# Attention by head pairs and transposes by row halves in a hybrid decoder step on one NeuronCore

## What is computed

```python
for layer in range(DEPTH):                                   # DEPTH = 2
    xp = layer_norm(ALPHA * xp + 0.5 * swiglu(xp, *f1), ...)  # xp prompt, xs samples, same weights
    if layer % 2 == 0:
        qa, ka, va, qb, kb, vb, gb = ab_project(xp, pos_p, w_in_ab[li])
        attn = moba_prompt(qa, ka, va, pos_p)      # per head: softmax(q k^T / 8 + causal mask) v
        attn_s = moba_sample(qa_s, ka_s, va_s, cache_k[li], cache_v[li], page_table, pos_s)
        ...                                        # retention, output projection
    else:
        mix_p, a_re, a_im = s5_layer(xp, ...)      # u: 64 groups x 16 channels, scan over time
    xp = layer_norm(ALPHA * xp + mix_p, ...)
    xp = layer_norm(ALPHA * xp + 0.5 * swiglu(xp, *f2), ...)
```

## Time and profile before

| what | value |
|---|---|
| time, median of 3 runs | 2546.82 us |
| lowest and highest | 2542.66 and 2546.82 us |
| the profiled execution's own time | 2551.39 us |
| its span, first to last instruction | 2549.4 us |
| TensorE busy, share of the span | 2436.4 us, 96% |
| VectorE, ScalarE, GpSimd | 64%, 43%, 18% |
| mean granted TensorE clock | 0.984 |
| DMA, mean | 164 GB/s |

### The profile page before, as it was taken

The page is one execution under the profiler, slowest core; times in us unless marked ns, Lnnn a source line. Parts: engine busy times, 40 slices in busy tenths (PEclk is TensorE's granted clock), DMA queues, the critical chain, the costliest instruction groups (busy, mean ns, idle before and its releaser), DMA issues.

```text
span 2549.4 us, 45472 instructions
## 1 busy us (share of the span) xinstructions
PE 2436.4 (96%) x18347; PEld 2287.9 (90%) x18347; DVE 1631.8 (64%) x2584; ACT 1085.4 (43%) x1645; POOL 457.9 (18%) x532
## 2 busy tenths in 40 slices
PE   7998999999999999999999999999999989999998
PEld 7988998998788767789999999999999889999997
DVE  5887776657665545577686657467656575486555
ACT  3433455333454333353253534455433537354333
POOL 4886700002100021300110201021001000121000
PEclk9999999999999999999899999999999999999999
DMA  8667776444354787644456556555555556555553
GB/s 178 177 176 191 196 198 191 132 122 118 113 152 122 231 256 238 176 124 135 118 169 188 155 150 190 184 160 151 149 152 144 168 173 211 154 154 148 153 150 98
DMA packets 676274, 417.26 MB, mean 164 GB/s; under 512 B 31554, under 2 KB 639682, under 8 KB 676066
## 3 DMA queue, kind: packets, MB, share of 16 engines
q1 hardware_dynamic: 669538, 393.98, 53.8%
q0 software_dynamic: 6528, 20.37, 2.6%
HBM read 395.51 MB, written 18.78 MB: 163 GB/s over the span
## 4 chain that ended last, share of the span: by engine, by line
PE 77%; DVE 12%; issue 3%; ACT 3%; SPq 2%; DMA 2%; POOL 0%; POOLq 0%; ACTq 0%; DVEq 0%
PE ps L256 20%; PE ps L258 19%; PE ps L257 19%; DVE w_lo L251 4%; PE ps L881 2%; PE ps L882 2%; PE ps L883 2%; ACT w_hi L242 2%; PE ps L2259 1%; PE ps L1582 1%; PE ps L1624 1%; PE ps L1597 1%; DMA w_raw<-in_ffn_w_up 1%; PE ps L1069 1%; SPq L1938 1%
## 5 line engine op out<-in xcount | busy, mean ns | idle before, releaser
L251 DVE TENSOR_TENSOR w_lo<-w_raw,w_hi 128x1024 fp32r<-128x1024 f32 (+1 forms) x648 | 823.2, 1275 | 631.3 <-ACT w_hi L242 628.5
L256 PE MATMUL ps<-x_hi,w_hi 128*128 128x256 f32 (+1 forms) x3200 | 968.0, 302 | 37.3 <-DVE w_lo L251 30.7
L257 PE MATMUL ps<-x_lo,w_hi 128*128 128x256 f32 (+1 forms) x3200 | 954.4, 298 | 0.0
L258 PE MATMUL ps<-x_hi,w_lo 128*128 128x256 f32 (+1 forms) x3200 | 954.3, 298 | 0.0
L242 ACT ACTIVATE w_hi<-w_raw 128x1024 fp32r<-128x1024 f32 (+1 forms) x648 | 669.2, 1034 | 540.0 <-PE ps L258 380.2
L256 PEld LDWEIGHTS ps<-x_hi,w_hi 128*128 128x128 f32 x3200 | 615.1, 192 | 54.5 <-DVE w_lo L251 40.7
L257 PEld LDWEIGHTS ps<-x_lo,w_hi 128*128 128x128 f32 x3200 | 615.4, 192 | 1.1 <-issue 0.2
L258 PEld LDWEIGHTS ps<-x_hi,w_lo 128*128 128x128 f32 x3200 | 614.7, 192 | 0.0
L256 PE MATMUL ps<-h_hi,w_hi 128*128 128x256 f32 (+1 forms) x1408 | 424.7, 302 | 13.8 <-DVE w_lo L251 10.9
L257 PE MATMUL ps<-h_lo,w_hi 128*128 128x256 f32 (+1 forms) x1408 | 414.8, 295 | 0.0
L258 PE MATMUL ps<-h_hi,w_lo 128*128 128x256 f32 (+1 forms) x1408 | 414.7, 295 | 0.0
(11 more groups left out here) (263 smaller groups left out, 2265.3 us busy)
## 6 DMA issues: line engine op xcount, KB each, us to landing
w_raw<-in_ffn_w_gate SPq DMA_DIRECT2D x176, 512.0 KB, 4.2
w_raw<-in_ffn_w_up SPq DMA_DIRECT2D x176, 512.0 KB, 3.9
w_raw<-in_ffn_w_down SPq DMA_DIRECT2D x128, 512.0 KB, 3.7
w_raw<-in_w_in_ab SPq DMA_DIRECT2D x56, 512.0 KB, 3.9
w_raw<-in_ffn_w_down SPq DMA_DIRECT2D x64, 384.0 KB, 3.3
arena<-in_cache_k SPq DMA_DIRECT2D x64, 256.0 KB, 3.7
arena<-in_cache_v POOLq DMA_DIRECT2D x64, 256.0 KB, 4.4
w_raw<-in_w_out_ab SPq DMA_DIRECT2D x16, 512.0 KB, 3.7
```

The source lines that it names most:

```text
L251: dve.tensor_tensor(T.w_lo[:, u % RING, 0:n], T.w_raw[:, u % RAW, 0:n], T.w_hi[:, u % RING, 0:n].bitcast(F32), ALU.subtract).then_inc(T.w_ ...
L256: pe.matmul(out, w_hi, m_hi, start=first, stop=False)
L257: pe.matmul(out, w_hi, m_lo, start=False, stop=False)
L258: return pe.matmul(out, w_lo, m_hi, start=False, stop=last)
```

## The change

Four things change; line numbers of the new kernel are given as L1056 and so on in the listings below.
- **Prompt attention by pairs.** A job is two heads (p) of one tile: 8 jobs and 11 steps for each of `att_a` and `att_b`. The two heads' scores stand one behind the other, on the two row halves, into banks `LOW` and `HIGH`. Every 128x128 turn of probabilities becomes two turns of 64 rows into `TURN` and `NORM_BANK`. Probabilities are held once, not twice; mask, maximum and shift are one VectorE instruction for both heads; the exponential and the move are two ScalarE instructions for a pair. A tile's output is turned into `LOW`, and the next scores, which need that bank, stand in the same step behind it.
- **Key pages by row halves.** A step turns its two pages together: 16 turns of 64 rows, alternating between the lower half (into `NORM_BANK`, moved by ScalarE) and the upper half (into `TURN`, moved by VectorE). It waits for both pages and for both moves of the step before. A slot is free when the step that turned it has ended.
- **S5 inputs by row halves.** 16 turns of 64 rows in place of 8, lower half into bank 4, upper into bank 5, and two ScalarE copies of half the size.
- **Samples' steps singly.** `slowly` in place of `paired`: of each 8 steps from step 8 on, the first four (softmax, turn of the probabilities, first values) stand behind an FFN step of their own, the other steps in twos. That makes 31 FFN steps in place of 22. As `att_b` takes 11 steps in place of 19, the samples now stand behind the 12th to the 42nd step of `f1a`; the first five of these are down steps.

```diff
--- before.py
+++ after.py
...
-        self.jobs = [(i, h) for i in tiles for h in range(HEADS)]
+        self.jobs = [(i, p) for i in tiles for p in range(PAIRS)]
         n = self.N = len(self.jobs)
...
-        k, r = divmod(s - lag - 2 - (HEADS - 1), HEADS)
+        k, r = divmod(s - lag - 2 - (PAIRS - 1), PAIRS)
...
-                if h == 0 and k:
+                if p == 0 and k:
...
+                for e in range(2):
+                    h = 2 * p + e
+                    for j in range(i + 1):
...
-                for j in range(self.jobs[n][0] + 1):
-                    mm = pe.transpose(T.ps[:, TURN, j * P:(j + 1) * P], self.prob[:, n % 2, j * P:(j + 1) * P],
-                                      T.ident[:, :])
+
+                for e in range(2):
+                    for j in range(self.jobs[n][0] + 1):
+                        for half in range(2):
+                            at = (4 * e + j) * HD
+                            mm = pe.transpose(T.ps[:, self.turns[half], at:at + HD],
+                                              self.prob[HALF[half], e, j * P:(j + 1) * P], T.ident[HALF[half], HALF[half]])
             k = self.last(s, 1)
             if k is not None:
                 pe.wait_ge(T.pa_normed.h, self.normed + k + 1)
                 pe.wait_ge(T.pa_expd.h, self.expd + min(s, self.N))
...
             if s < self.N:
-                i, h = self.jobs[s]
-                if s >= 2:
-                    pe.wait_ge(T.pa_expd.h, self.expd + s - 1)
-                k = self.last(s - 1, 1)
+                i, p = self.jobs[s]
+                if s:
+                    pe.wait_ge(T.pa_expd.h, self.expd + s)
                 if k is not None and self.put is None:
                     pe.wait_ge(T.pa_rested.h, self.rested + k + 1)
                 elif k is not None:
                     pe.wait_ge(T.pa_rounded.h, self.rounded + k + 1)
-                rows = HALF[h % 2]
-                pe.matmul(T.ps[:, LOW + s % 2, 0:(i + 1) * P], M.qaT[self.g][rows, h // 2, local(self.g, i)],
-                          M.kaT[rows, h // 2, 0:(i + 1) * P], start=True, stop=True).then_inc(T.pa_scored.h, 1)
+                for e in range(2):
+                    mm = pe.matmul(T.ps[:, LOW + e, 0:(i + 1) * P], M.qaT[self.g][HALF[e], p, local(self.g, i)],
+                                   M.kaT[HALF[e], p, 0:(i + 1) * P], start=True, stop=True)
+                mm.then_inc(T.pa_scored.h, 1)
...
+            if s < self.N:
+                i = self.jobs[s][0]
+                two = slice(2 * s, 2 * s + 2)
+                dve.wait_ge(T.pa_scored.h, self.scored + s + 1)
+                diag = T.ps[:, LOW:LOW + 2, i * P:(i + 1) * P]
+                T.dve_chain(dve, dve.tensor_tensor(diag, diag, M.causal[:, :].unsqueeze(1).to_broadcast([P, 2, P]), ALU.add))
+                T.dve_chain(dve, dve.tensor_reduce(self.top[:, two], T.ps[:, LOW:LOW + 2, 0:(i + 1) * P], AX_X, ALU.max))
+                dve.tensor_scalar(self.shift[:, two], self.top[:, two], -HD ** -0.5, None, ALU.mult)\
+                   .then_inc(T.pa_maxed.h, 1)
...
+                tiles = slice(0, self.jobs[n][0] + 1)
                 act.wait_ge(T.pa_turned.h, self.turned + n + 1)
-                if n >= 2:
-                    act.wait_ge(T.pa_valued.h, self.valued + n - 1)
-                act.activation(self.prob_t[:, n % 2, 0:w], T.ps[:, TURN, 0:w], ACT.Copy).then_inc(T.pa_moved.h, 1)
+                if n:
+                    act.wait_ge(T.pa_valued.h, self.valued + n)
+                for half in range(2):
+                    last = act.activation(
+                        self.prob_t.rearrange("p e (j h t) -> p h e j t", h=2, t=HD)[:, half, :, tiles],
+                        T.ps[:, self.turns[half], :].rearrange("p (e j t) -> p e j t", e=2, t=HD)[:, :, tiles], ACT.Copy)
+                last.then_inc(T.pa_moved.h, 1)
...
                 act.wait_ge(T.pa_maxed.h, self.maxed + s + 1)
-                if s >= 2:
-                    act.wait_ge(T.pa_turned.h, self.turned + s - 1)
-                act.activation(self.prob[:, s % 2, 0:w], T.ps[:, LOW + s % 2, 0:w], ACT.Exp,
-                               bias=self.shift[:, s:s + 1], scale=HD ** -0.5, accum_out=self.total[:, s:s + 1])\
-                   .then_inc(T.pa_expd.h, 1)
+                if s:
+                    act.wait_ge(T.pa_turned.h, self.turned + s)
+                for e in range(2):
+                    at = slice(2 * s + e, 2 * s + e + 1)
+                    last = act.activation(self.prob[:, e, 0:w], T.ps[:, LOW + e, 0:w], ACT.Exp, bias=self.shift[:, at],
+                                          scale=HD ** -0.5, accum_out=self.total[:, at])
+                last.then_inc(T.pa_expd.h, 1)
...
             if i >= slots:
-                q.wait_ge(T.sa_k_turned.h, i - slots + 1)
+                q.wait_ge(T.sa_k_turned.h, (i - slots) // 2 + 1)
             q.dma_start(self.k_slots[i % slots], src).then_inc(self.k_slot_loaded[i % slots].h, 16)
...
-    def turn_keys(self, pe, i):
+    def turn_keys(self, pe, s):
+
         T = self.T
         slots = len(self.k_slots)
-        pe.wait_ge(self.k_slot_loaded[i % slots].h, (i // slots + 1) * 16)
-        if i >= 2:
-            pe.wait_ge(T.sa_k_moved[i % 2].h, i // 2)
+        for i in (2 * s, 2 * s + 1):
+            pe.wait_ge(self.k_slot_loaded[i % slots].h, (i // slots + 1) * 16)
+        if s:
+            for moved in T.sa_k_moved:
+                pe.wait_ge(moved.h, s)
         for p in range(PAIRS):
-            mm = pe.transpose(T.ps[:, (NORM_BANK, TURN)[i % 2], p * P:(p + 1) * P],
-                              self.k_slots[i % slots][:, p * P:(p + 1) * P], T.ident[:, :])
+            for i in range(2):
+                for half in range(2):
+                    at = (i * PAIRS + p) * HD
+                    mm = pe.transpose(T.ps[:, (NORM_BANK, TURN)[half], at:at + HD],
+                                      self.k_slots[(2 * s + i) % slots][HALF[half], p * P:(p + 1) * P],
+                                      T.ident[HALF[half], HALF[half]])
...
-            for i in (2 * s, 2 * s + 1):
-                if i < BP * 2 * PAGES:
-                    self.turn_keys(pe, i)
-            yield
-
-    def move_keys(self, eng, copy, i):
+            if s < BP * PAGES:
+                self.turn_keys(pe, s)
+            yield
...
+    def move_keys(self, eng, copy, s, half):
+
         T = self.T
-        b, r = divmod(i, PAGES)
+        b, r = divmod(2 * s, PAGES)
         b2, j = divmod(r, GP)
         if b:
             eng.wait_ge(T.sa_scored.h, b)
-        eng.wait_ge(T.sa_k_turned.h, i + 1)
-        copy(self.keys[:, b2, :, j * P:(j + 1) * P],
-             T.ps[:, (NORM_BANK, TURN)[i % 2], :].rearrange("p (a t) -> p a t", a=PAIRS))\
-            .then_inc(T.sa_k_moved[i % 2].h, 1)
+        eng.wait_ge(T.sa_k_turned.h, s + 1)
+        copy(self.keys[:, b2].rearrange("p a (j h t) -> p h j a t", h=2, t=HD)[:, half, j:j + 2],
+             T.ps[:, (NORM_BANK, TURN)[half], :].rearrange("p (j a t) -> p j a t", j=2, a=PAIRS))\
+            .then_inc(T.sa_k_moved[half].h, 1)
...
-            if 2 * s + 1 < BP * 2 * PAGES:
-                self.move_keys(dve, dve.tensor_copy, 2 * s + 1)
+            if s < BP * PAGES:
+                self.move_keys(dve, dve.tensor_copy, s, 1)
...
-            if 2 * s < BP * 2 * PAGES:
-                self.move_keys(act, lambda out, src: act.activation(out, src, ACT.Copy), 2 * s)
+            if s < BP * PAGES:
+                self.move_keys(act, lambda out, src: act.activation(out, src, ACT.Copy), s, 0)
...
                 for t in range(CL):
-                    mm = pe.transpose(T.ps[0:c, 4 + t // 4, (t % 4) * P:(t % 4 + 1) * P],
-                                      T.x[:, e, g.cols.start + t:g.cols.stop:CL], T.ident[:, :])
+                    for half in range(2):
+                        mm = pe.transpose(T.ps[0:c, 4 + half, t * HD:(t + 1) * HD],
+                                          T.x[HALF[half], e, g.cols.start + t:g.cols.stop:CL],
+                                          T.ident[HALF[half], HALF[half]])
                 mm.then_inc(S.chunk_turned.h, 1)
...
-                copy(self.chunked[e % 2][0:c].rearrange("p k t h -> p t k h"),
-                     T.ps[0:c, 4:6, :].rearrange("p b (t k h) -> p (b t) k h", t=4, h=GH)).then_inc(S.chunk_moved.h, 1)
+                for half in range(2):
+                    last = copy(self.chunked[e % 2][0:c, half * A4:(half + 1) * A4].rearrange("p k t h -> p t k h"),
+                                T.ps[0:c, 4 + half, :].rearrange("p (t k h) -> p t k h", t=CL, h=GH))
+                last.then_inc(S.chunk_moved.h, 1)
...
+        def slowly(steps):
+
+            return paced(steps, [s for s in range(AttendSamples.STEPS) if s >= 8 and s % 8 < 4])
...
-            weave(ffn(ffn_sync, sp, f1a), after(after(idle(att_b.STEPS - 4), samples.begin(sp)), paired(samples.sync(sp))))
```

(3 more changed lines are left out.)

39 lines of the change are left out of this document (13 added, 26 removed).

## The result

The changed kernel takes 2531.17 us (median of 5, 2527.69 to 2534.42), the kernel before 2546.82 us (median of 5, 2542.66 to 2547.19). The ratio is 0.9935, 95% interval 0.9917 to 0.9953: 15.7 us less, where the prediction said 34. It lies just outside the range of 2496 to 2530, 1 us above its upper end, and the kernel got faster, as was forecast.

What follows compares the result with a forecast made beforehand. The prediction took TensorE, busy for 96% of the span, as mostly the bound. Its terms, -11.9 - 3.6 - 3.1 + 3.3 - 7.5 - 5.1 - 6.2 = -34.1 us, took 2546.8 to 2512.7, forecast as 2513, range 2496 to 2530.

Steps and rivals of the forecast that it cites:

- a to d, prompt attention: Prompt attention: paired scores -11.9, half turns of probabilities -3.6, 16 fewer insertions -3.1, an added wait +3.3 us.
- e, key turns: Samples' key pages: 256 turns by halves save 11.5 us, shape changes and more insertions cost 4.0, together -7.5.
- f, S5 inputs: S5 inputs: 128 turns by halves save 5.8 us, changes of shape cost 0.7, together -5.1.
- g, the samples' pace: Samples' attention: with single steps, 9.5 of 15.7 us of waits and low clock remain, -6.2, between -15.7 and +7.
- The price of a half turn: TensorE: a pair of half turns costs 0.064 us, 0.045 saved per full turn; 16 half turns in about 0.55 us.
- the rival of the weight loads: Weight loads keep a pair at a full turn's 0.109 us, so probability and key turns save nothing: 2528 us, chance 0.07.
- that of the halves one after the other: The row halves do not overlap, a pair costs 0.128 us and the 464 turns lose 8.8: 2542 us, chance 0.04.
- The added wait (d): Prompt attention: scores behind a finished tile wait until the output bank is read, 1.8 + 1.5 us, +3.3.
- these waits lie where the softmax chain or the moved probabilities are needed within the same pair of steps: Samples' attention: the step claiming that FFN steps of their own cover the present waits, 15.7 us with the low clock.
- no fall of the clock near the first samples' softmax: Samples' attention: a sign expected in the profile after; before, the granted clock was 0.72 and 0.60 between 890 and 900.
- The rival of the late pages: Samples' key turns: ten FFN steps with two key steps together all wait for pages, 59 us: about 2562, chance 0.05.
- the S5 inputs stand ahead of that scan, so what they save still counts: Second S5 group: though VectorE is busy 54.5 of 60 us in the scan, the inputs' saving ahead of it counts.

Runs made afterwards that it cites:

- e1: The kernel before with the prompt attention by pairs alone, eight empty side steps keeping the samples at their old FFN steps: 2531.57 us, ratio 0.9939.
- e2: The kernel before with the key pages by row halves alone, samples still in twos: 2547.29 us, ratio 0.9999.
- e7: The changed kernel with the samples' exponentials on ScalarE and their sum on VectorE one side step later: 2519.80 us, ratio 0.9901 against the kernel before.
- e11: e7 with the key pages turned by full 128x128 turns as in the kernel before: 2523.33 us, ratio 0.9913 against the kernel before.
- e3: The kernel before with the S5 inputs by row halves alone: 2548.06 us, ratio 1.0000.
- e12: e9 with the second half of the first values held until eight steps of keys are turned, not four: 2515.34 us, ratio 0.9881 against the kernel before.
- e9: e7 with a GpSimd wait that holds the samples' first 2 MB of values until four key steps are turned: 2517.53 us, ratio 0.9887 against the kernel before.

## Why the prediction was wrong

| term | forecast | shown |
|---|---|---|
| a to d, prompt attention | -15.3 | -15.5 (e1, interval -19 to -12) |
| e, key turns | -7.5 | -0.3 alone (e2, -3 to +3); -3.5 with the exponentials moved (e7 against e11) |
| f, S5 inputs | -5.1 | 0 by the times (e3, -3 to +3); -1.4 by the profiles, all in group A |
| g, the samples' pace | -6.2 | about +6.5 by the waits and the clock (below); the single steps alone -1.8 (medians), -3.3 (ratios) or -6.3 (`f1a`) |

**The price of a half turn was right.** Sixteen take 0.55 us, as the prediction put it, so neither the rival of the weight loads (0.9) nor that of the halves one after the other (1.0) holds; that the time came out 3 us from the first rival's 2528 is chance. TensorE's row for the weight loads of the first 16 says the same, 16 loads of 128 columns with 0.57 us from the start of the first to the end of the last:

```profile
786.23 0.57 PEld L1614 LDWEIGHTS ps<-ident,arena 64*128 64x128 f32 x16
```

By the Trainium skill, page "TensorE: Matmul & The Clock Gate", section "LDWEIGHTS (loading the stationary operand)", a load takes its columns divided by 1.2 GHz whatever its rows; an estimate from that figure is 1.7 us for these 16 one behind the other, by which half turns would be dearer than full ones and not, as the prediction read it, equal to them. The trace does not agree for loads of 64 rows on alternating halves, 0.57 us for the 16, and the measurement decides.

**The prompt attention was right in sum, and partly by another way.** The added wait (d) is 1.50 us behind tile 0 and 1.17 behind tile 2, for 1.8 and 1.5. Before, the retention behind `att_a` waited for VectorE; the waits of 560 to 616 in the kernel before are

```profile
PE ps L1220 <- DVE arena L1213: 2.5, 2, 1.8
```

and at the same place in the changed kernel and in e1 there are none; the retention now begins eight steps earlier, which is the likely reason, not tested by itself. The prediction has no such term, so that its sum of 15.3 met the 15.5 so closely is in part luck.

**Where it failed is the step "these waits lie where the softmax chain or the moved probabilities are needed within the same pair of steps; given FFN steps of their own, they are covered".** It asked only who waits for the samples' chain. It did not ask what stands behind that chain on VectorE and ScalarE: the rounding of the FFN's weights and its gate. TensorE got an FFN step to work on, and then that FFN step's own supply was late. The chain from the first maximum to the last exponential is 824.5 to 830.4, longer than a gate/up step of 5.8 us, and ScalarE and VectorE take 3.4 us more to catch up. For the prompt attention the prediction had held its 4 us chain against 5.8 and found cover; the samples' chain it never measured. e7 shows the cause: with the same work, and ScalarE free to round weights while VectorE is at the chain, 7 to 9 us come back (11 by the medians against the changed kernel). What is queued behind a moved step the prediction had asked of SP, and not of ScalarE. Of the signs that it named, the one that failed points here: "no fall of the clock near the first samples' softmax", where the clock fell to 0.50.

**In the sum this is term g, which has the wrong sign.** The prediction kept 9.5 us of waits for the samples, for pages and copies alone. By TensorE's list these are 10.8 us, near enough; what it put at nothing is 6.1 at the gate (3.9 in the first pair of samples, 1.1 in each of two later ones) and 0.4 for values, and the low clock behind the two gaps, 4.9 us from 795 to 805 and 830 to 845, reckoned as the prediction did for the kernel before. That makes 22.2 where it kept 9.5 and where the kernel before had 15.7: +6.5 in place of -6.2. With the 7 to 8 us of work that the half turns of keys took out, as term e had it, it leaves the 1 us by which `f1a` differs from e1. The rival of the late pages had the right place and the wrong extent: two waits of 3.6 and 2.7 us in the second side step, as "what would show it" had said, and not ten. With the exponentials moved and the values held back (e12), `f1a` is 13.4 us shorter than in the changed kernel, and the ratio puts the time at 2516.5 on the prediction's base of 2546.8; the 3.8 left to its 2512.7 is what the S5 inputs did not bring, within an interval of 5 us either way.

**The S5 term was right per step and had nothing behind it in the end.** In group A, six steps save 0.24 us each and the other two nothing: 1.4 in all. In group B the stage is as long as before, 164.3 us both from the same FFN product ahead of the input steps to the same one behind them, and the last input step starts 85.5 us behind that first product in both, so the saving is gone before the scan begins. The first input steps there stand behind the norm, whose work on VectorE and ScalarE sets when the next weights are rounded and the gate begins (L410):

```profile
1966.62 1.95 ACT L563 ACTIVATE x<-x,ln_bias 128x320 f32<-128x320 f32 x4 [3.92 <-DVE x L531]
...
1968.26 0.64 PE L2248 MATMUL ps<-ident,x 64*40 64x64 f32 x16
1968.47 1.04 ACT L242 ACTIVATE w_hi<-w_raw 128x1024 fp32r<-128x1024 f32 x1
1969.53 1.28 ACT L410 ACT_TABLE_LOAD   x1
...
1970.83 0.38 ACT L410 ACTIVATE gate<-ps 128x256 f32<-128x256 f32 x1
```

TensorE's turns are 0.4 us shorter here and the table load of 1.28 us ahead of the gate is as long as before; TensorE waits instead. Two such waits come to 3.0 us, for the weights' remainder, where before there was none at these places, and behind the second the granted clock is 0.55 and 0.59 from 1980 to 1988 (before, it fell at these two places to 0.76 and 0.63); the later six steps win back 0.35 each. The sentence "the S5 inputs stand ahead of that scan, so what they save still counts" looked at the scan behind them and not at the norm ahead of them. This is read from profiles; no run moves the norm.

**What stays open.** Key turns alone are worth 4 us by the stretch of one profile and nothing by 11 timed runs. That the single execution profiled of the kernel before ran 4.6 us over its median makes every difference from it too large: its stretch 255 to 270, which the change does not touch, took some 4 us longer than in the other profiles. What the single steps alone are worth lies between 2 and 6 us. What holds the input steps of S5 group B to the same length is not tested.

## What to carry to other kernels

Two products of 64 rows on the two row halves ran beside each other here, and a 128x128 transpose cut into two halves cost 0.062 us in place of 0.109; where TensorE is the bound, as in the prompt attention, that is real time. Before side work is given more room on TensorE, list what stands behind it on VectorE and ScalarE: an engine that waits at a softmax cannot feed the FFN, and moving ScalarE's part of the softmax one step later was worth more here, 7 to 9 us, than all the half turns of keys and S5 inputs, some 5. Let an engine wait for a chain only where the chain is done by then, and hold bulk loads back with a semaphore, not by their place in a program that nothing slows.

## What the hardware showed beyond that

The two half turns of a pair start 3 to 4 ns apart and the pairs 62 ns, with 128 weight columns loaded for each. A page of 256 KB landed in 3.8 us (median) where the values are held back (e9), and in 7.2 us beside their 2 MB (the changed kernel), with the DMAs at a share of 1.06 and 373 GB/s. The gap at the gate cost more than its own length: behind the one of 4 us at 830 (1.05 of 5 us busy) the next 5 us, all busy, were granted 0.50, which is 2.5 us more.
